# Dealing the glu's two products out between the units of prompt attention

## Chip, cores and metric

The kernel runs on one core of a Trainium2 chip. The metric is the device time of one execution in microseconds (us), the median of several runs. TensorE's clock is granted at one of two levels, 1.2 and 2.4 GHz; the profile writes it as 0.50 and 1.00.

## The reference

Two layers run, one after the other. Each layer handles a prompt of 512 tokens and 8 sample tokens (520 columns in all) with the same weights: a feed-forward half step, the token mixing, and a second half step. The change is in the mixing, which is this:

```python
y_a = (y_ssm @ glu_w) * jax.nn.sigmoid(y_ssm @ glu_v)              # 512 -> 1024 features
attn = attention_fn(q, k, v, q_idx, k_idx, w_idx)
y_b = attn.reshape(bsz, t_len, D_ATT) @ w_branch_attn              # 512 -> 1024 features
mixed = (jax.nn.sigmoid(gate_a) * y_a + jax.nn.sigmoid(gate_b) * y_b) @ w_out
```

`y_ssm` is there before attention begins. Prompt attention is over 512 tokens and 8 heads of 64, with an indexer that keeps the best 128 keys of each query. Sample attention is over 2048 cached keys, of which 256 are gathered for each sample.

## The kernel before

All activations are feature major: 128 features on the partitions, 520 tokens along the row, in two halves of 260 columns (one PSUM bank each; the tile `PS` is four pairs of banks). An fp32 product `x @ w` is made of three fp32r products, hi*hi, hi*lo and lo*hi. Weights come in chunks through a ring of four slots: SyncE loads `stage` (`load`), ScalarE writes `w_hi`, VectorE writes the rest `lo_over` in place of `stage` (the two `split` functions, L714 and L1569), and TensorE's `tile` uses them. A slot is free again when TensorE has used the chunk four before (`chunk_used`). All orders are written out by hand: each engine has its own program, and semaphores tie them.

The mixing's stages, in the order of time: projections and the state space model (its outputs `y_hi`, `y_lo`, the gates in `gT`), the v product, the index scores and the choice of keys, prompt attention, the tail of sample attention, the glu and branch stage, the output projection `wo`.

Prompt attention has 32 units n: four query tiles t of 128 tokens by eight heads, with t + 1 key tiles. TensorE's order (L1503 on) is `logits(n + 2)` (`PS<-kT,qT`), `turn_scaled(n)` (`PS<-dgr,ex`, the transposed, scaled weights), `values(n - 1)` (`PS<-pT,vP`). VectorE does `lowered` (mask and maximum, L2192) and `scaled_diagonal` (`dgr`, L2202), ScalarE `exps` (L998) and the copy `turned_out` (`pT`, L1006). Beside eight of the units (`sample_beside`, n = 6, 9, ... 27) VectorE multiplies gathered keys of one sample by that sample's query (`key_logits`, `prk`, L2177), which TensorE has spread over all partitions with one fp32 matmul into PSUM pair 3 (`spread_query`, `PS<-q_s,pick`).

The glu and branch stage begins at `att_s_ready`, when the sample's attention rows are done; SyncE then also reloads `xT` (2 MB) from memory. In each of eight output blocks there are three tiles of 24 matmuls, glu_w, glu_v and branch:

```python
for v in range(12):
    ...
    tile(v % 4, [(chunk('glu', v, i, 12), 0, KD // 2, P)], (h_hi, h_lo) if v % 3 == 2 else (y_hi, y_lo),
         first=KD // 2 if v % 3 == 2 else 0)
```

ScalarE takes the sigmoid of the glu_v tile (L1040), VectorE makes the four elementwise steps (L2277 to L2285), ScalarE rounds the sum to `mx_hi` (L1043) and VectorE writes `mx_lo` (L2289). The output projection waits for all eight `mx_lo`.

## Time and profile before

| | |
|---|---|
| median of 3 runs | 3499.21 us (3491.34 to 3499.61) |
| the profiled execution | 3497.53 us, its span 3495.8 us |
| TensorE matmul busy | 2979.6 us, 85% of the span |
| VectorE, ScalarE, GpSimd busy | 47%, 37%, 10% |
| granted TensorE clock, mean | 0.888 |
| prompt attention, layer one | 1036.5 to 1146.4 us |
| tail of sample attention | 1146.4 to 1173.8 us |
| glu and branch | 1173.8 to 1252.7 us |

The profile is that of one execution. PE is TensorE, DVE VectorE, ACT ScalarE, POOL GpSimd and SP SyncE. Matmuls overlap in their records, so two that start 0.24 us apart can each be listed with 0.28 us; the start to start distance is what a group costs. An fp32 matmul is two records. In a row of the timeline, what stands in brackets is the idle time of the engine before it and who ended it.

### The profile page before, as it was taken

The numbers are of one execution on the slowest core, as the hardware profiler recorded it, in microseconds if no ns is written. First come the engines' busy times: TensorE is split into PE (matmuls) and PEld (weight loads), VectorE is DVE, ScalarE is ACT, GpSimd is POOL, SyncE is SP. The second block draws the span as 40 slices with busy tenths as digits, with TensorE's granted clock in tenths as the row PEclk, the third lists the DMA queues.
The fourth block names the chain that finished last, engine by engine and source line by source line (L and its number), as shares of the span: only waits on it lengthen the run. The fifth ranks groups of instructions, "written<-read, shape, count | busy, mean of one in ns | idle before, by whom it ended". The sixth has DMA issues, their size and how long they took to land. (4 is left out here: it accounts for less than half of the span.)

```text
span 3495.8 us, 56227 instructions
## 1 busy us (share of the span) xinstructions
PE 2979.6 (85%) x21838; PEld 2754.9 (79%) x21838; DVE 1650.8 (47%) x3202; ACT 1276.4 (37%) x2050; POOL 332.7 (10%) x309
## 2 busy tenths in 40 slices
PE   5999996698839987999769999957887499799996
PEld 4899996687715787999759999957886257789996
DVE  4542446665385444323464424476644844443234
ACT  5542334334252234322165323243443422343221
POOL 2000002032031101000010000020320310100000
PEclk8999997899956998999879999978998579899998
DMA  7443533122201332232164435330221113322321
GB/s 230 123 148 103 156 100 123 31 55 55 74 18 38 114 99 61 84 97 83 38 206 145 144 109 155 97 114 26 54 61 62 30 37 116 86 73 84 100 79 52
DMA packets 450149, 319.80 MB, mean 91 GB/s; under 512 B 24841, under 2 KB 403073, under 8 KB 449210
## 3 DMA queue, kind: packets, MB, share of 16 engines
q1 hardware_dynamic: 444570, 292.37, 28.2%
q0 software_dynamic: 5408, 25.17, 2.3%
q8 instruction: 105, 1.72, 0.2%
q14 instruction: 66, 0.54, 0.1%
HBM read 306.28 MB, written 11.21 MB: 91 GB/s over the span
## 5 line engine op out<-in xcount | busy, mean ns | idle before, releaser
L1067 PE MATMUL PS<-h_hi,w_hi 128*128 128x260 f32 (+1 forms) x4000 | 838.2, 291 | 41.3 <-DVE h_lo L1637 35.0
L1067 PE MATMUL PS<-h_lo,w_hi 128*128 128x260 f32 (+1 forms) x4000 | 816.3, 286 | 0.0
L1569 DVE TENSOR_TENSOR lo_apart<-stage,w_hi 128x1024 fp32r<-128x1024 f32 (+2 forms) x448 | 495.4, 1141 | 467.2 <-ACT w_hi L714 459.6
L1067 PEld LDWEIGHTS PS<-h_hi,w_hi 128*128 128x128 f32 (+1 forms) x4000 | 631.8, 192 | 63.1 <-issue 39.6
L1067 PEld LDWEIGHTS PS<-h_lo,w_hi 128*128 128x128 f32 (+1 forms) x4000 | 628.2, 192 | 0.0
L714 ACT ACTIVATE w_hi<-stage 128x1024 fp32r<-128x1024 f32 (+3 forms) x586 | 541.1, 955 | 96.5 <-DMA stage<-in_mod_w 33.0
L1067 PE MATMUL PS<-h_hi,lo_apart 128*128 128x260 f32 x2816 | 568.7, 284 | 0.0
L1067 PEld LDWEIGHTS PS<-h_hi,lo_apart 128*128 128x128 f32 x2816 | 436.9, 189 | 0.0
L1067 PE MATMUL PS<-hid_lo,w_hi 128*128 128x260 f32 x1408 | 286.2, 285 | 0.0
L1067 PE MATMUL PS<-hid_hi,w_hi 128*128 128x260 f32 x1408 | 285.6, 284 | 0.0
L1067 PE MATMUL PS<-hid_hi,lo_apart 128*128 128x260 f32 x1408 | 285.2, 284 | 0.0
L1685 DVE TENSOR_TENSOR hidf<-sil,PS 128x520 f32<-128x520 f32 x88 | 61.3, 696 | 406.2 <-PE PS L1067 406.2
L1067 PE MATMUL PS<-h_hi,lo_over 128*128 128x260 f32 (+1 forms) x1184 | 248.0, 292 | 0.0
L789 ACT ACTIVATE hid_hi<-hidf 128x520 f32 (+1 forms) x88 | 56.2, 639 | 466.1 <-DVE hidf L1685 466.1
L1067 PEld LDWEIGHTS PS<-hid_hi,lo_apart 128*128 128x128 f32 x1408 | 219.4, 190 | 0.0
L1067 PEld LDWEIGHTS PS<-hid_hi,w_hi 128*128 128x128 f32 x1408 | 219.3, 190 | 0.1
L1067 PEld LDWEIGHTS PS<-hid_lo,w_hi 128*128 128x128 f32 x1408 | 219.2, 190 | 0.0
L1569 DVE TENSOR_TENSOR lo_over<-stage,w_hi 128x1024 fp32r<-128x1024 f32 (+1 forms) x138 | 143.0, 1041 | 130.1 <-ACT w_hi L714 129.1
L1067 PEld LDWEIGHTS PS<-h_hi,lo_over 128*128 128x128 f32 (+1 forms) x1184 | 191.7, 197 | 0.0
L2324 POOL COPY ssum<-sq 128x520 f32<-128x520 f32 x6 | 6.5, 1085 | 1694.0 <-ACT sq L729 1694.0
L1067 PE MATMUL PS<-w_hi,c_st 128*128 128x512 f32 x288 | 127.6, 443 | 18.8 <-DVE lo_apart L1569 11.3
L783 ACT ACTIVATE sil<-PS 128x520 f32<-128x520 f32 x88 | 53.2, 605 | 199.3 <-PE PS L1067 199.1
(408 smaller groups left out, 4058.0 us busy)
## 6 DMA issues: line engine op xcount, KB each, us to landing
stage<-in_ffn_in SPq DMA_DIRECT2D x176, 512.0 KB, 4.0
stage<-in_mod_w SPq DMA_DIRECT2D x144, 512.0 KB, 4.8
stage<-in_w_in SPq DMA_DIRECT2D x72, 512.0 KB, 3.8
stage<-in_ffn_out SPq DMA_DIRECT2D x64, 384.0 KB, 3.7
stage<-in_ffn_out SPq DMA_DIRECT2D x64, 320.0 KB, 3.5
stage<-in_w_out SPq DMA_DIRECT2D x16, 512.0 KB, 4.0
x_hold<-xT SPq DMA_DIRECT2D x2, 2080.0 KB, 6.8
xT<-x_hold SPq DMA_DIRECT2D x2, 2080.0 KB, 8.9
```

What stands on the lines that cost most here:

```text
L714: nc.scalar.activation(w_hi[:, ch.slot, 0:ch.elems], stage[:, ch.slot, 0:ch.elems], ACT.Copy)\
L783: nc.scalar.activation(sil[:, m, :].rearrange("p (a n) -> p a n", a=2), PS[:, 2 * m, :, 0:HALF], ACT.Silu).then_inc(ev_a, 1)
L789: nc.scalar.activation(hid_hi[:, bass.ds(i * 2 + m, 1), :], hidf[:, m:m + 1, :], ACT.Copy)\
L1067: return nc.tensor.matmul(out, lhsT, rhs, start=start, stop=stop)
L1569: nc.vector.tensor_tensor(lows(ch)[:, ch.slot, 0:ch.elems], stage[:, ch.slot, 0:ch.elems], w_hi[:, ch.slot, 0:ch.elems].bitcast(FP32), ALU ...
L1685: nc.vector.tensor_tensor(hidf[:, m, :].rearrange("p (a n) -> p a n", a=2), sil[:, m, :].rearrange("p (a n) -> p a n", a=2), PS[:, up, :, ...
L2324: pool.tensor_copy(ssum[:], sq[:, 0, :]).then_inc(sq_added, 1)
```

## The change

The chunk phase 'glu' keeps only the two glu weights (16 chunks), and a new phase 'br' has the 8 branch chunks. After each attention unit n TensorE runs `fill(n)`: one half (260 columns) of one of the two products of block n // 4, 12 matmuls, into PSUM pair 3. Units 4m and 4m + 1 make the product with glu_w, units 4m + 2 and 4m + 3 that with glu_v, into the same two banks. VectorE multiplies the first into `gT` (`gated_by_gate`, in unit 4m + 2), ScalarE takes the sigmoid of the second (`sigmoids`, in unit 4m + 4), VectorE multiplies that in as well (`gated_by_sigmoid`, in unit 4m + 5). The splits of the chunks stand in the even units. The queries of the samples no longer go through TensorE: SyncE writes `q_s` to memory and reads each row back, spread over the partitions, into `qb`. SyncE's loads of the first four glu chunks stand ahead of the outputs of the states. The branch stage has eight tiles with three elementwise steps each. Besides, some semaphores are merged and one increment (`hf_ready`) goes.

```diff
-            ('glu', 24, 4 * P, 8, 16), ('wo', 8, BLK, 8, 0),
+            ('glu', 16, 4 * P, 0, 0), ('br', 8, 4 * P, 0, 8), ('wo', 8, BLK, 8, 0),
...
+                def glu_pair(m):
+                    for q, name in enumerate(('glu_w', 'glu_v')):
+                        load(chunk('glu', 2 * m + q), rows_of(name, 0, KD // 2, m * P, P))
+
                 def out(name, src, view, sent=out_done):
                     sp.dma_start(view(io[name][lds]), src).then_inc(sent, 16)
 
+                glu_pair(0)
+                glu_pair(1)
...
+                sp.dma_start(q_hold, q_s[:]).then_inc(q_held, 16)
+
+                def query(b):
+                    if b >= 4:
+                        sp.wait_ge(kg_used, b - 3)
+                    sp.dma_start(qb[:, b % 4, :], q_hold[b:b + 1, :].partition_broadcast(P)).then_inc(qb_in[b % 4], 16)
+
+                sp.wait_ge(gi_ready, 1)
+                sp.wait_ge(q_held, 16)
+                for b in range(4):
+                    query(b)
+                glu_pair(2)
+                glu_pair(3)
+                for m in range(4, KD):
+                    query(m)
+                    glu_pair(m)
...
-                def branches(i):
-                    for m in range(4):
-                        for q, name in enumerate(('glu_w', 'glu_v', 'w_branch_attn')):
-                            load(chunk('glu', 3 * m + q, i, 12), rows_of(name, 0, KD // 2, (i * 4 + m) * P, P))
-                        if type(i) is int and i == m == 0:
-                            sp.wait_ge(att_s_ready, 1)
-                            sp.dma_start(xT[:].rearrange("p k n -> p (k n)"), x_hold).then_inc(x_back, 16)
-                branches(0)
-                branches(1)
+                sp.wait_ge(att_s_ready, 1)
+                sp.dma_start(xT[:].rearrange("p k n -> p (k n)"), x_hold).then_inc(x_back, 16)
+                for m in range(3, KD):
+                    branch(m)
...
+                def sigmoids(m):
+                    act.wait_ge(chunk_used, chunk('glu', 2 * m + 1).number(1))
+                    if m:
+                        act.wait_ge(part_ready, m)
+                    nc.scalar.activation(sg[:], PS[:, 3, :, 0:HALF], ACT.Sigmoid).then_inc(sig_ready, 1)
+
                 exps(0)
                 for n in range(NU):
                     if n + 1 < NU:
                         exps(n + 1)
                     turned_out(n)
+                    if n % 2 == 0:
+                        split(chunk('glu', n // 2 + 2))
+                    if n % 4 == 0 and n:
+                        sigmoids(n // 4 - 1)
                     if n % H == 2 and n > H:
                         attended(n // H - 1)
                 attended(TT - 1)
+                sigmoids(KD - 1)
...
-                        act.wait_ge(ev_d, i * 8 + (evicts_d['glu'] + 2 * (m - 1)))
-                        nc.scalar.activation(tmpn[:, m % 2, :].rearrange("p (b n) -> p b n", b=2),
-                                             PS[:, (3 * m + 1) % 4, :, 0:HALF], ACT.Sigmoid).then_inc(ev_a, 1)
...
+                for m in range(KD):
+                    split(chunk('br', m + 2))
+                    act.wait_ge(mixf_ready, m + 1)
+                    nc.scalar.activation(mx_hi[:, m:m + 1, :], sq[:, m % 2:m % 2 + 1, :], ACT.Copy).then_inc(mx_hi_ready, 1)
...
-                def spread_query(b):
-
-                    if b >= 2:
-                        pe.wait_ge(kg_used, b - 1)
-                    mm(PS[:, 3, b % 2, :], pick[:, b, :], q_s[:]).then_inc(qb_done, 1)
+                def fill(f):
+                    m, q = divmod(f, 4)
+                    which, half = q // 2, q % 2
+                    ch = chunk('glu', 2 * m + which)
+                    if which:
+                        pe.wait_ge(glu_used, m + 1)
+                    elif m:
+                        pe.wait_ge(sig_ready, m)
+                    pe.wait_ge(lo_done, ch.number(1))
+                    for k in range(KD // 2):
+                        for w, x in ((w_hi, y_hi), (w_hi, y_lo), (lows(ch), y_hi)):
+                            last = mm(PS[:, 3, half, 0:HALF], w[:, ch.slot, k * P:(k + 1) * P], x[:, k, half * HALF:(half + 1) * HALF],
+                                      start=(k == 0 and w is w_hi and x is y_hi), stop=(k == KD // 2 - 1 and w is not w_hi))
+                    if half:
+                        last.then_inc(chunk_used, 1)
...
+                    fill(n)
                 values(len(units_) - 1)
 
                 pe.wait_ge(att_lo, TT)
+                pe.wait_ge(sig_ready, KD)
...
-                with pe.Fori(0, 2) as i:
-                    ea, ed = evicts_a['glu'], evicts_d['glu']
-                    for v in range(12):
-                        pe.wait_ge(ev_a, i * 4 + (ea + (v - 2) // 3))
-                        pe.wait_ge(ev_d, i * 8 + (ed + (v - 4) // 3 + (v - 6) // 3 + 2))
-                        tile(v % 4, [(chunk('glu', v, i, 12), 0, KD // 2, P)], (h_hi, h_lo) if v % 3 == 2 else (y_hi, y_lo),
-                             first=KD // 2 if v % 3 == 2 else 0)
+                for v in range(KD):
+                    if v >= 4:
+                        pe.wait_ge(ev_d, evicts_d['br'] + v - 3)
+                    tile(v % 4, [(chunk('br', v), 0, KD // 2, P)], (h_hi, h_lo), first=KD // 2)
...
-                    dve.wait_ge(qb_done, b + 1)
-                    nc.vector.tensor_tensor(prk[:], kv[b % K_BUFS][:], PS[:, 3, b % 2, :].unsqueeze(1).to_broadcast([P, 2, DA]), ALU.mult)\
+                    dve.wait_ge(qb_in[b % 4], 16 * (b // 4 + 1))
+                    nc.vector.tensor_tensor(prk[:], kv[b % K_BUFS][:], qb[:, b % 4, :].unsqueeze(1).to_broadcast([P, 2, DA]), ALU.mult)\
...
+                def gated_by_gate(m):
+                    dve.wait_ge(chunk_used, chunk('glu', 2 * m).number(1))
+                    g = halves_of(gT[:, m:m + 1, :])
+                    nc.vector.tensor_tensor(g, g, PS[:, 3, :, 0:HALF], ALU.mult).then_inc(glu_used, 1)
+
+                def gated_by_sigmoid(m):
+                    dve.wait_ge(sig_ready, m + 1)
+                    dve.wait_ge(glu_used, m + 1)
+                    g = halves_of(gT[:, m:m + 1, :])
+                    nc.vector.tensor_tensor(g, g, sg[:], ALU.mult).then_inc(part_ready, 1)
+
                 lowered(0)
                 for n in range(TT * H):
                     if n + 1 < TT * H:
                         lowered(n + 1)
                     scaled_diagonal(n)
+                    if n % 2 == 0:
+                        split(chunk('glu', n // 2 + 2))
+                    if n % 4 == 2:
+                        gated_by_gate(n // 4)
+                    if n % 4 == 1 and n > 4:
+                        gated_by_sigmoid(n // 4 - 1)
                     if n in sample_beside:
                         key_logits(sample_beside[n])
                     if n % H == 4 and n > H:
                         attended(n // H - 1)
                 attended(TT - 1)
+                gated_by_sigmoid(KD - 1)
...
+                for m in range(KD):
+                    split(chunk('br', m + 2))
+                    dve.wait_ge(chunk_used, chunk('br', m).number(1))
+                    nc.vector.tensor_tensor(hf[:, m % 2, :].rearrange("p (b n) -> p b n", b=2), PS[:, m % 4, :, 0:HALF],
+                                            halves_of(gT[:, m + KD:m + KD + 1, :]), ALU.mult).then_inc(ev_d, 1)
+                    dve.wait_ge(ev_d, evicts_d['br'] + m + 1)
+                    dve.wait_ge(part_ready, KD)
+                    nc.vector.tensor_tensor(sq[:, m % 2], hf[:, m % 2], gT[:, m, :], ALU.add).then_inc(mixf_ready, 1)
+                    dve.wait_ge(mixf_ready, m + 1)
+                    dve.wait_ge(mx_hi_ready, m + 1)
+                    nc.vector.tensor_tensor(mx_lo[:, m:m + 1, :], sq[:, m % 2:m % 2 + 1], mx_hi[:, m:m + 1, :].bitcast(FP32),
+                                            ALU.subtract).then_inc(mx_lo_ready, 1)
+
```

In the rows of the order that follow, L numbers of "now" are lines of the changed file. ScalarE in prompt attention, units 2 to 5 of t = 0: `ex` is `exps`, `pT` is `turned_out`, `w_hi` a split, `sg` the sigmoid. Before:

```order
L998 ACTIVATE ex,att_140<-lg,att_140 128x128 [waits pt_turned,neg_ready]
L1006 ACTIVATE pT<-PS 128x128 [waits pv_done,pt_turned]
L998 ACTIVATE ex,att_140<-lg,att_140 128x128 [waits pt_turned,neg_ready]
L1006 ACTIVATE pT<-PS 128x128 [waits pv_done,pt_turned]
L998 ACTIVATE ex,att_140<-lg,att_140 128x128 [waits pt_turned,neg_ready]
L1006 ACTIVATE pT<-PS 128x128 [waits pv_done,pt_turned]
```

Now:

```order
L1031 ACTIVATE pT<-PS 128x128 [waits pv_done,pt_turned]
L741 ACTIVATE w_hi<-stage 128x512 [waits chunk_used,stage_full1]
L1042 ACT_TABLE_LOAD
L1042 ACTIVATE sg<-PS 128x520 [waits chunk_used]
L1023 ACT_TABLE_LOAD [waits pt_turned]
L1023 ACTIVATE ex,att_140<-lg,att_140 128x128 [waits neg_ready]
L1031 ACTIVATE pT<-PS 128x128 [waits pv_done,pt_turned]
```

The split, the sigmoid and two table loads now stand between one unit's `pT` and the next but one `ex`. There are eight sigmoids in each layer's attention, each with a load before it, and a load before the exp that follows.

VectorE at unit 6, where the gate product and the first sample's keys meet: `dgr` is the end of `scaled_diagonal`, `prk` the keys by the query. Before:

```order
L2199 RECIPROCAL att_140<-att_140 128x1 [waits ex_ready]
L2202 TENSOR_SCALAR dgr<-ident,att_140 128x128 [waits pt_turned,dve_own]
L2175 ISA
L2177 TENSOR_TENSOR prk<-kv_163,PS 128x1024 [waits qb_done,k_in0]
L2180 TENSOR_REDUCE Lg<-prk 128x16 [waits kg_used]
```

Now:

```order
L2227 RECIPROCAL att_140<-att_140 128x1 [waits ex_ready]
L2230 TENSOR_SCALAR dgr<-ident,att_140 128x128 [waits pt_turned,dve_own]
L1597 TENSOR_TENSOR lo_over<-stage,w_hi 128x512 [waits hi_done]
L2243 TENSOR_TENSOR gT<-gT,PS 128x520 [waits chunk_used]
L2203 ISA
L2205 TENSOR_TENSOR prk<-kv_163,qb 128x1024 [waits qb_in0,k_in0]
L2208 TENSOR_REDUCE Lg<-prk 128x16 [waits kg_used]
```

The split and the gate product now stand behind the diagonal and ahead of the keys; `prk` reads its query from `qb` and no longer from PSUM.

TensorE at unit 4: `kT,qT` is `logits`, `dgr,ex` is `turn_scaled`, `pT,vP` is `values`, and the rows with `y_hi` or `y_lo` begin a fill. Before:

```order
L1067 MATMUL PS<-kT,qT 128x128 [waits neg_ready]
L1067 MATMUL PS<-dgr,ex 128x128 [waits pt_ready,dgr_ready]
L1067 MATMUL PS<-pT,vP 64x128 [waits pt_ready]
L1067 MATMUL PS<-kT,qT 128x128 [waits neg_ready]
L1067 MATMUL PS<-dgr,ex 128x128 [waits pt_ready,dgr_ready]
```

Now:

```order
L1091 MATMUL PS<-kT,qT 128x128 [waits neg_ready]
L1091 MATMUL PS<-dgr,ex 128x128 [waits pt_ready,dgr_ready]
L1091 MATMUL PS<-pT,vP 64x128 [waits pt_ready]
L1091 MATMUL PS<-y_hi,w_hi 128x260 [waits lo_done,sig_ready]
L1091 MATMUL PS<-y_lo,w_hi 128x260
L1091 MATMUL PS<-y_hi,lo_over 128x260
```

Twelve matmuls now stand behind each values group; the first of a unit 4m waits for the sigmoid of the block before, that of a unit 4m + 2 for the gate product (`glu_used`).

## Rows read from the trace of the kernel before

**Rows 1.** Windows: start:end, length, busy us (records) of five engines, PEclk, DMA share, GB/s

```profile
1036.50:1108.00 71.50, 70.67 (x191) 40.79 (x190) 33.83 (x122) 18.95 (x66) 14.72 (x16) 0.50 0.21 59
1108.00:1146.40 38.40, 36.99 (x209) 24.29 (x207) 20.77 (x61) 14.61 (x34) 5.67 (x6) 0.99 0.15 42
...
1173.80:1252.70 78.90, 72.09 (x576) 71.89 (x577) 45.92 (x67) 28.61 (x45) 0.00 (x0) 0.93 0.41 124
2770.60:2842.30 71.70, 70.88 (x191) 40.77 (x190) 33.82 (x122) 18.95 (x66) 14.68 (x16) 0.50 0.20 59
```

**Rows 2.** Timeline (start us, us, engine, line, what), two units t = 0 apart

```profile
2777.86 0.79 PE L1067 MATMUL PS<-kT,qT 64*128 64x128 f32 x2
...
2779.93 0.79 PE L1067 MATMUL PS<-kT,qT 64*128 64x128 f32 x2
```

**Rows 3.** Timeline of TensorE, a unit of t = 1 and a spread query

```profile
1066.58 1.22 PE L1067 MATMUL PS<-kT,qT 64*128 64x256 f32 x2
...
1069.93 2.07 PE L1067 MATMUL PS<-q_s,pick 8*128 8x512 f32 x2
```

**Rows 4.** Timeline at the high clock, a unit of t = 3 with its pT

```profile
1136.78 1.12 PE L1067 MATMUL PS<-kT,qT 64*128 64x512 f32 x2
...
1138.92 1.09 PE L1067 MATMUL PS<-pT,vP 128*64 128x128 f32 x8
...
1139.03 0.60 ACT L1006 ACTIVATE pT<-PS 128x512 f32<-128x512 f32 x1 [1.86 <-PE PS L1067]
...
1139.94 1.16 PE L1067 MATMUL PS<-dgr,ex 128*128 128x128 f32 x8
```

**Rows 5.** Timeline of the glu stage's matmuls, at either clock

```profile
1174.86 0.80 PE L1067 MATMUL PS<-y_hi,w_hi 128*128 128x260 f32 x2 [1.53 <-DVE lo_over L1569]
...
1179.79 0.64 PE L1067 MATMUL PS<-y_hi,lo_over 128*128 128x260 f32 x2
...
1180.22 0.64 PE L1067 MATMUL PS<-y_hi,w_hi 128*128 128x260 f32 x2
...
1183.11 0.40 PE L1067 MATMUL PS<-y_hi,lo_over 128*128 128x260 f32 x2
...
1183.35 0.40 PE L1067 MATMUL PS<-h_hi,w_hi 128*128 128x260 f32 x2
```

**Rows 6.** Windows of 4 us in the stage of the gates

```profile
836.00:840.00 4.00, 2.18 (x28) 1.93 (x28) 3.86 (x14) 0.00 (x0) 0.00 (x0) 1.00 0.00 0
840.00:844.00 4.00, 2.11 (x14) 2.02 (x13) 3.39 (x10) 3.58 (x9) 3.45 (x3) 0.86 0.52 135
```

**Rows 7.** Timeline of TensorE there, the matmul behind the gap

```profile
837.82 0.67 PE L1067 MATMUL PS<-CA,BXl 128*32 128x128 f32 x16 [3.58 <-DVE counting L1795]
```

**Rows 8.** Timeline of the glu stage, a split and the product behind it

```profile
1200.72 0.63 ACT L714 ACTIVATE w_hi<-stage 128x512 fp32r<-128x512 f32 x1 [2.11 <-DMA stage<-in_glu_v]
...
1201.38 0.69 DVE L1569 TENSOR_TENSOR lo_over<-stage,w_hi 128x512 fp32r<-128x512 f32 x1 [2.05 <-ACT w_hi L714]
1201.99 0.69 DVE L2277 TENSOR_TENSOR hf<-tmpn,PS 128x520 f32<-128x520 f32 x1
```

**Rows 9.** Timeline of ScalarE, a table load and the activation behind it

```profile
1174.61 1.28 ACT L714 ACT_TABLE_LOAD   x1
...
1175.91 0.63 ACT L714 ACTIVATE w_hi<-stage 128x512 fp32r<-128x512 f32 x1
```

**Rows 10.** Timeline of VectorE, a sample's keys

```profile
1129.66 1.21 DVE L2177 TENSOR_TENSOR prk<-kv,PS 128x1024 f32<-128x1024 f32 x1
```

**Rows 11.** Timeline of VectorE in the glu stage, sum, mx_lo and split

```profile
1204.53 0.70 DVE L2285 TENSOR_TENSOR sq<-hf 128x520 f32<-128x520 f32 x1
1206.01 0.70 DVE L2289 TENSOR_TENSOR mx_lo<-sq,mx_hi 128x520 fp32r<-128x520 f32 x1 [0.78 <-ACT mx_hi L1043]
1206.62 1.32 DVE L1569 TENSOR_TENSOR lo_over<-stage,w_hi 128x512 fp32r<-128x512 f32 x2
```

**Rows 12.** Timeline of ScalarE, the first glu chunk behind the reload of x

```profile
1183.24 1.38 ACT L714 ACTIVATE w_hi<-stage 128x512 fp32r<-128x512 f32 x2 [6.70 <-DMA stage<-in_glu_w]
```

136 lines of the change are left out of this document (52 added, 84 removed).

## Prediction

> **What bounds the kernel now.** I read the page's busy shares first (TensorE 85%, in the table ahead, so every stage is first asked for its TensorE time), then the windows of the stages that the change touches, then their instructions in order of time. Prompt attention runs 32 units (four query tiles t = 0 to 3, eight heads), and in it TensorE's records leave no gap: 70.67 of 71.50 us, then 36.99 of 38.40 [rows 1]. But in the first 71.5 us the granted clock is 0.50, the level of 1.2 GHz, and only then 0.99, that of 2.4 GHz; layer two shows the same (71.7 us at 0.50). The stage of glu and branch is 78.9 us with 576 matmuls, at 0.93. So the change moves 384 of 576 matmuls out of a dense stage into one that has no TensorE gap to fill, but half of which runs at the low level. Three questions decide: does the clock rise earlier, what do the added handoffs cost, and how short is what is left of the branch stage?
>
> **Prices on TensorE.** At 1.2 GHz a unit of t = 0 (logits, transposing product, values) takes 2.07 us [rows 2], one of t = 1 1066.58 to 1069.93 = 3.35 us [rows 3]. The difference of 1.28 us is the columns of one key tile, the rest, 0.79 us, the starts of three groups. At 2.4 GHz a unit of t = 3 takes 3.16 us [rows 4]: columns at half price, 4 x 0.64 = 2.56, leave 0.60 for the starts. So a unit costs 0.64(t+1) + 0.60 at the high level. All 32: 8 x (0.64 x 10 + 4 x 0.60) = **70.4 us**. A fill is 12 of the glu's matmuls. Two of them take 0.43 us at the low level and 0.24 at the high one [rows 5], so a fill is 2.60 or **1.44 us**, 32 fills 83 or **46 us**. The spread queries go: 2.07 us each by the record at the low level [rows 3], eight per layer, of which two stand before the first unit.
>
> **The clock.** In the branch stage it rose 5.6 us after dense matmuls of this very shape began (1174.86; the pair at 1179.79 still takes 0.43 us, that at 1183.11 0.24 [rows 5]). In attention it stayed low for 71 us, with group starts that take 0.79 of 2.07 us. A fill is 2.60 us without such gaps, and then 2.07 us with them. I take the rise in the first two units. They then cost 2 x 2 us more less what is hidden: 3.2 us. Does it fall again at the handoffs? From 836 to 840 TensorE is busy 2.18 of 4 us at 1.00 [rows 6], just behind an idle gap of 3.58 us [rows 7], and the clock falls only in the next four (0.86). My gaps are 1.6 to 2.5 us with at least 5 us of work between. I let it stay up.
>
> **Two handoffs in every four units.** Both glu products use the same two PSUM banks, so a fill has to wait for who empties them.
> (1) The fill of unit 4m+2 waits for VectorE's product with the gate. VectorE has put a split ahead of that, which waits for ScalarE's half of the split, which stands behind the copy pT of the same unit, which waits for TensorE's transposing product. From the start of the values group: pT starts 0.11 us later [rows 4], takes 0.28 to 0.60; ScalarE's split adds 0.57, VectorE's 0.61 (1201.38 to 1201.99), the product 0.69 [rows 8], and 0.07 to TensorE: 2.05 + pT. The values group covers 0.38, 0.59, 0.80 or 1.02 us of it. Left: 1.95, 1.84, 1.74, 1.63; two of each: **14.3 us**.
> (2) The fill of unit 4m waits for the sigmoid, which stands behind pT, the split and a table load. The load takes 1.28 us, and the next activation starts 1.30 us after it [rows 9]. From the start of the values group: 0.11 + pT + 0.57 + 1.30 + 0.60 + 0.05 = 2.63 + pT, less the values group: 2.2 to 2.6, mean 2.4; seven of them: **17 us**. The second load (back to exp) lies beside the fill and the next logits and costs nothing; if that cover went it would be 1.3 us each.
> On these two waits everything on TensorE is queued, the next logits first. VectorE's sample keys (1.21 us for the product and as much for the sum [rows 10]) come right behind the gate product in units 6 and 18, and near it in two others: 3.7 us of late diagonals. Start and end of the stage as before: 1.3 + 1.4 us. The last sigmoid with its table load: 1.2 us more before the sample's softmax, and 0.7 us for VectorE's product behind it.
>
> Attention then: 70.4 + 46 + 14.3 + 17 + 3.7 + 1.3 + 1.4 + 1.2 + 3.2 = **158.5 us**; before, 1036.5 to 1146.4 = 109.9 [rows 1]. That is **+48.6** per layer, +0.7 behind it, and -0.2 because VectorE waits a little less for the first logits.
>
> **The branch stage** is 8 tiles of 24 matmuls, 2.9 us each. VectorE is slower. Per tile: product to sum 0.73 us (0.70 and a start), sum to mx_lo (with ScalarE's mx_hi between, VectorE idle 0.78) 1.48, mx_lo to split 0.61 [rows 11], split to product 0.61 [rows 8]: **3.43 us**. Tile 0 starts at 1173.9 at 1.2 GHz and is done at 1179.1. The fourth chunk is queued behind the reload of x. In before the chunk that was queued there was split only at 1183.24, after 6.70 us of waiting for it [rows 12]. I take the same: the second product at 1184.5, the last one 6 x 3.43 + 1.8 (two chunks of twice the size) later at 1206.9, its mx_lo ended 2.9 us after: 1209.8. The output projection begins there, before it began at 1252.7: **-42.8**, and +0.8 since TensorE has then been idle some 8 us and starts low (before, a shorter gap). Bounds: TensorE alone would need 23 + 2.6 + 2.9 = 28.5 us, another 7.5 less; a chunk that comes 3 us late adds 3.
>
> **Without price.** Queries by DMA: 16 KB out and eight broadcasts of 256 KB, asked for one to four keys ahead, while DMA stands at 0.21 [rows 1]; an arrival late by 1 us would cost 1 us in eight units. SP is moved: two glu pairs now stand ahead of the outputs of states, and wait until the last chunk of v is used. VectorE waits for these outputs only after ScalarE has copied v out and TensorE has turned the keys, so they have that time to land; bounds 0 and 2 us per layer, I take 0. Chunks 4 to 15 are asked for some two units (5 us and more) before ScalarE splits them. The split of the first four is in the v stage, where VectorE and ScalarE idle. The fp32 activation merges and renamed semaphores change nothing.
>
> **Sum.** Per layer 48.6 + 0.7 - 0.2 - 42.8 + 0.8 = +7.1 us, two layers +14.2. Profiled execution 3497.5 + 14.2 = 3511.7; the median of before stands 1.7 above that execution, so **3513 us**. What I cannot read from the trace: a fill may also pay a group's start (0.2 x 32 = +6.4 per layer), the logits behind it may lose theirs (-6.4), the handoffs may be 0.2 us off each (3), the branch chain 3. Own range 3498 to 3530.
>
> **Rivals.**
> A. The forecast, 68%.
> B. The clock does not rise with the first fills. Per unit that costs 4.67 - 2.68 = 2.0 us at t = 0 and 2.6 at t = 1. Low through t = 0: +12 per layer, 3537; through t = 1: +29, 3571. For it: 71 us at 0.50 under unbroken records. Against: what broke them were group starts, and fills have none. 14%.
> C. A table change costs more than its row. The row shows 1.28 us and no gap around it [rows 9]. 5%, +19 us for seven exposed changes in two layers, 3532; that price is bounded by a second load of the same length in each.
> The Trainium skill ("ScalarE: Activation LUTs", What ACT_TABLE_LOAD costs) says that exp and sigmoid sit in different sets, that a change is 1.28 us and a drain of 1.38 besides, and that activations are to be batched by set, which this change undoes. The row agrees with 1.28 and shows no drain.
> D. Faster. TensorE loads the weights of the fp32 groups behind a fill, so the 0.60 us of starts per unit vanish: 32 x 0.60 x 2 = 38 us, 3475. It decides above 0.36 us per unit (forecast to 10.5 us below the median). For it: only starts stop TensorE in [rows 2 to 4]. Against: two of the three groups in a unit still follow an fp32 group, and each waits for a semaphore. 6%.
> The Trainium skill ("TensorE: Matmul & The Clock Gate", Part 2, step by step) has the queue pull weight loads ahead of running matmuls when row groups don't conflict or the background buffer is free, which would favour D; the starts in [rows 2 to 4] do not show it between fp32 groups.
> E. The freed slots come too late and each of chunks 4 to 15 is waited for by 1 us (glu chunks were waited for by 2.11 us in the old stage [rows 8]): +24, 3537. 7%.
>
> **Chances.** A measurement of this kernel tells 0.3%, 10.5 us, from no change. A lies within it with 25 of its 68 points and above with 43. Faster 6 (D), same 25, slower 43 + 14 + 5 + 7 = 69. For 8 in 10 the range goes from 3490 to 3560: D below and the worse half of B above are left out.
>
> **What will show it.** Right: clock near 1.0 from the first units; ScalarE with 14 more table loads per layer; TensorE idle in attention some 35 us per layer, on the gate product (1.8 each) and on the sigmoid (2.4 each); attention 159 us; from the sample's last row to the output projection 36 us, VectorE's step 3.4 us. Wrong: a clock of 0.50 beyond 15 us, stalls on stage loads, or handoffs under 1.3 us, which would mean that ScalarE and VectorE run ahead of where I put them.

## The result and the profile after

The changed kernel takes **3554.9 us** (median of 4 runs, 3550.3 to 3558.2) against 3495.8 us for the kernel before beside it (4 runs, 3491.3 to 3499.6): a ratio of 1.0168, 95% interval 1.0149 to 1.0188, 59 us slower. The forecast was 3513 us: right in direction, inside the wide range (3490 to 3560) but outside the prediction's own one (3498 to 3530), and 42 us short in size.

The profiled execution of the changed kernel has a span of 3553.0 us, before 3495.8. First the windows of layer one, of the kernel after; they answer to [rows 1] (start:end, length, busy us and records of TensorE, its weight loads, VectorE, ScalarE, GpSimd; granted clock, DMA share, GB/s). The first is prompt attention from VectorE's first logits to the first matmul behind the last unit, then four stretches of it, then the branch stage.

```profile
1034.90:1219.00 184.10, 148.76 (x765) 115.30 (x765) 73.32 (x213) 67.79 (x140) 19.95 (x22) 0.82 0.21 64
1040.00:1058.00 18.00, 13.71 (x62) 10.76 (x63) 5.38 (x24) 5.64 (x15) 0.95 (x1) 0.77 0.26 87
1058.00:1074.00 16.00, 14.15 (x56) 10.61 (x55) 6.93 (x20) 4.25 (x13) 1.90 (x2) 0.63 0.17 50
1074.00:1119.00 45.00, 36.65 (x161) 29.21 (x160) 18.07 (x49) 15.57 (x32) 3.79 (x4) 0.69 0.20 59
1119.00:1219.00 100.00, 79.95 (x476) 60.93 (x475) 40.27 (x107) 40.16 (x73) 9.48 (x10) 0.94 0.18 53
...
1246.00:1284.00 38.00, 25.07 (x196) 23.86 (x197) 23.18 (x35) 11.39 (x18) 0.00 (x0) 0.91 0.46 147
```

The same window of the kernel before, first logits to first matmul behind, is this:

```profile
1037.30:1146.40 109.10, 106.86 (x394) 64.57 (x393) 54.05 (x181) 33.56 (x100) 19.86 (x21) 0.67 0.19 54
```

So attention went from 109.1 to 184.1 us: **+75.0**, where the prediction had +49.3 (48.6, and 0.7 behind the last unit). TensorE's records leave 35.3 us open, as forecast. What was not forecast stands in the last columns: the clock is at 1.00 in none of the first three stretches. Over the 184 us its mean is 0.82; the levels are 0.5 and 1, so about 2 x 0.18 x 184 = 66 us were spent at the low one.

The waits of TensorE on the two handoffs, over the whole execution (waiting line <- releaser: us in total, times, longest us), the changed kernel:

```profile
PE PS L1091 <- ACT sg L1042: 34.4, 14, 3.1
...
PE PS L1091 <- DVE gT L2243: 27.0, 16, 1.9
...
PE PS L1091 <- DVE mx_lo L2325: 16.9, 2, 8.5
```

That is 2.46 us for each sigmoid and 1.69 for each gate product; the prediction had 2.4 and 1.8. The handoffs were sized right. What follows on them was not. TensorE in layer one of the changed kernel, at the first handoffs (start us, us, engine, line, what, idle before):

```profile
1048.01 0.39 PE L1091 MATMUL PS<-y_hi,w_hi 128*128 128x260 f32 x1 [1.85 <-DVE gT L2243]
1048.23 0.28 PE L1091 MATMUL PS<-y_lo,w_hi 128*128 128x260 f32 x1
1048.35 0.32 PE L1091 MATMUL PS<-y_hi,lo_over 128*128 128x260 f32 x1
1048.47 0.42 PE L1091 MATMUL PS<-y_hi,w_hi 128*128 128x260 f32 x1
1048.69 0.42 PE L1091 MATMUL PS<-y_lo,w_hi 128*128 128x260 f32 x1
...
1052.33 0.39 PE L1091 MATMUL PS<-y_hi,w_hi 128*128 128x260 f32 x1
1052.55 0.28 PE L1091 MATMUL PS<-y_lo,w_hi 128*128 128x260 f32 x1
1052.67 0.28 PE L1091 MATMUL PS<-y_hi,lo_over 128*128 128x260 f32 x1
```

Behind 1.85 us of idle time a fill begins at 0.12 us per matmul, and with its fourth matmul the step is 0.22: the clock has fallen to the low level. At 1052.33 it is high again, and behind the next handoff it falls once more. Counted fill by fill over layer one, 16 of 32 fills run at the high level through (about 1.64 us each), 13 with at least nine of their twelve matmuls at the low one (up to 2.90), 3 in between; all 32 take 69.0 us, where the prediction had 46 and two low ones.

The branch stage, from its first matmul to the output projection, and VectorE's chain in it, of the changed kernel:

```profile
1246.83 0.51 PE L1091 MATMUL PS<-h_hi,w_hi 128*128 128x260 f32 x2 [0.51 <-DVE h_lo L2311]
...
1283.68 0.80 PE L1091 MATMUL PS<-mx_hi,w_hi 128*128 128x260 f32 x2 [8.45 <-DVE mx_lo L2325]
```

```profile
1262.36 0.70 DVE L2322 TENSOR_TENSOR sq<-hf,gT 128x520 f32<-128x520 f32 x1
1263.83 0.70 DVE L2325 TENSOR_TENSOR mx_lo<-sq,mx_hi 128x520 fp32r<-128x520 f32 x1 [0.78 <-ACT mx_hi L1069]
1264.45 0.69 DVE L1597 TENSOR_TENSOR lo_over<-stage,w_hi 128x512 fp32r<-128x512 f32 x1
1265.06 0.69 DVE L2318 TENSOR_TENSOR hf<-PS,gT 128x520 f32<-128x520 f32 x1
1265.78 0.70 DVE L2322 TENSOR_TENSOR sq<-hf,gT 128x520 f32<-128x520 f32 x1
```

36.9 us instead of the 78.9 of [rows 1], and a step of 3.42 us from sum to sum (1262.36 to 1265.78). TensorE is idle for 8.45 us ahead of the output projection.

From the first logits to the output projection the two layers take 215.4 and 215.1 us before, 248.8 and 248.0 after: 33 us more in each. All the rest together is 9 us shorter; the start of attention lay between 1030.4 and 1040.4 us in the profiles of all the kernels below, so a few us of that are no effect of a kernel.

### The profile page after: what moved, and what is told of

Read it like the earlier page. It is cut to its first block and busy times, and to the rows that moved or that the text cites. A ratio compares the mean times of both kernels' runs of the same rounds, so it can differ in the third digit from the quotient of the medians.

```text
span 3553.0 us, 56157 instructions
## 1 busy us (share of the span) xinstructions
PE 2956.0 (83%) x21806; PEld 2752.0 (77%) x21806; DVE 1647.3 (46%) x3202; ACT 1314.9 (37%) x2078; POOL 334.1 (9%) x309
## 5 line engine op out<-in xcount | busy, mean ns | idle before, releaser
L1091 PE MATMUL PS<-y_hi,w_hi 128*128 128x260 f32 x256 | 94.1, 367 | 61.4 <-ACT sg L1042 34.4
L1091 PE MATMUL PS<-w_hi,c_st 128*128 128x512 f32 x288 | 127.2, 442 | 18.1 <-DVE lo_apart L1597 10.6
```

What stands on the lines that cost most here:

```text
L1091: return nc.tensor.matmul(out, lhsT, rhs, start=start, stop=stop)
```

## Experiments

Theory 1: the missing 42 us are the granted clock, which falls because TensorE stands idle at the handoffs, and then takes several us of dense work to rise. Theory 2, its rival: the clock is low because of the short fp32 groups of t = 0 and 1, as it was before [rows 1], and the handoffs only stand beside it; then no repair of the handoffs brings it back. Every ratio is against the kernel before, run beside it. On the chips used, that kernel's median lay between 3489.6 and 3495.8 us, so a difference between two runs can be off by up to 6 us in their times; where it matters, it is also given by the ratios (0.01 is 35 us).

**Without handoffs.** The fills stay, nobody empties their banks.

```diff
                 def fill(f):
-                    if which:
-                        pe.wait_ge(glu_used, m + 1)
-                    elif m:
-                        pe.wait_ge(sig_ready, m)
                     pe.wait_ge(lo_done, ch.number(1))
...
-                    if n % 4 == 0 and n:
-                        sigmoids(n // 4 - 1)
...
-                    if n % 4 == 2:
-                        gated_by_gate(n // 4)
-                    if n % 4 == 1 and n > 4:
-                        gated_by_sigmoid(n // 4 - 1)
...
```

> The changed kernel with the fills of attention left in place and split, but nobody empties their two banks between them: the seven sigmoids and the products with gate and sigmoid of the first seven pairs are left out, and so are the waits for them. All 384 matmuls, the splits and the loads are still there. Theory 1 (the granted clock falls because TensorE stands idle at the handoffs): the direct gaps go (34 + 27 us for both layers in the waits, 31 per layer) and so do the falls of the clock, some 22 us per layer; attention 183 -> about 130 us, kernel about 3449 us. Theory 2 (the clock is low because of the group starts of the short units, as in the first 71 us of attention before; the handoffs only stand beside it): only the gaps go, attention about 152 us, kernel about 3493 us, and the clock still falls to 0.50 in the units t = 0 and 1.

Measured 3483.0 us (7 runs, 3468.1 to 3490.4), ratio 0.9962 (0.9947 to 0.9977); attention 147.8 us at a mean clock of 0.90. Neither number came. Fills 2 to 6 are all at the high level, which speaks against theory 2, but then TensorE stops for another reason. TensorE, and what VectorE did in that time, of this run:

```profile
1062.96 0.70 PE L1087 MATMUL PS<-kT,qT 64*128 64x256 f32 x2
1066.30 0.79 PE L1087 MATMUL PS<-dgr,ex 128*128 128x128 f32 x2 [2.64 <-DVE dgr L2222]
...
1067.64 0.58 PE L1087 MATMUL PS<-y_hi,w_hi 128*128 128x260 f32 x1
1068.02 0.42 PE L1087 MATMUL PS<-y_lo,w_hi 128*128 128x260 f32 x1
```

```profile
1061.90 0.69 DVE L1589 TENSOR_TENSOR lo_over<-stage,w_hi 128x512 fp32r<-128x512 f32 x1 [3.37 <-ACT w_hi L741]
1062.51 1.22 DVE L2197 TENSOR_TENSOR prk<-kv,qb 128x1024 f32<-128x1024 f32 x1
1063.77 1.22 DVE L2200 TENSOR_REDUCE Lg<-prk 128x16 f32<-128x1024 f32 x1
```

VectorE waits 3.37 us for ScalarE's split, which stands behind pT of the same unit, and then does split, a sample's product and its sum in one go: 3.1 us. The diagonal `dgr`, without which TensorE cannot transpose, is 2.64 us late, and the fill behind it is at the low level (0.22 per matmul). In the changed kernel the handoffs hid this third wait.

**The gaps filled.** All handoffs stay; TensorE does useless matmuls while it waits.

```diff
                     ch = chunk('glu', 2 * m + which)
+                    if half == 0 and f:
+                        for _ in range(12 if which else 20):
+                            mm(PS[:, 1, (f + 1) % 2, 0:HALF], y_hi[:, 0, 0:P], y_hi[:, 1, 0:HALF])
                     if which:
```

> The changed kernel with every handoff kept, and the idle time filled: ahead of each of the 15 waits TensorE runs matmuls of the fill's own shape that nobody uses, 12 before the wait for the gate product (1.44 us at the high clock), 20 before the wait for the sigmoid (2.4 us), into a bank that is free there. Theory 1: the clock stays at 1.00 once it has risen, and the low stretches, some 22 us per layer, go: attention 183 -> about 161 us, kernel about 3511 us although more work is done. Theory 2: nothing is gained, since the waits end when they did: 3555 us, or up to 20 us more where the added matmuls run past the wait at the low clock.

Measured **3521.3 us**, ratio 1.0080 (1.0063 to 1.0097): 33.6 us less than the changed kernel (31 by the ratios), with 236 more matmuls per layer (1001 against 765) and no handoff taken away. Windows of this run:

```profile
1034.90:1046.00 11.10, 10.32 (x40) 8.51 (x40) 3.47 (x20) 2.96 (x12) 4.76 (x6) 0.54 0.66 234
1046.00:1066.00 20.00, 19.57 (x131) 16.37 (x130) 9.01 (x28) 7.75 (x19) 0.59 (x1) 1.00 0.14 41
1066.00:1074.00 8.00, 6.68 (x27) 4.56 (x25) 2.19 (x11) 2.02 (x7) 1.30 (x2) 0.69 0.42 128
1074.00:1201.10 127.10, 122.21 (x807) 98.68 (x807) 58.23 (x155) 55.40 (x104) 13.27 (x14) 0.99 0.20 59
```

The clock rises in the first 11 us and stays but for one dip, behind a diagonal 1.32 us late. That shows theory 1: the idle time itself costs what TensorE cannot do in it, and some 17 us per layer more. (The expectation was 3511; the dip and matmuls that run past the end of a wait may be the 10 us, which was not separated.)

**Only the sigmoid's gaps filled** (the same edit with `and not which`).

> As the run that filled every gap, but only the seven gaps per layer at the sigmoid (2.2 to 3.0 us) are filled, with 20 matmuls each; the eight at the gate product (1.5 to 1.9 us) stay idle. If the falls of the clock come from the long gaps alone, this gives all that filling both gave: 3521 us, and the clock is high behind the gate's gaps. If gaps of 1.5 to 1.9 us make it fall as well, the falls at t = 0 and 1 stay in part: 3530 to 3550 us.

Measured 3523.4 us, ratio 1.0096 (1.0079 to 1.0112): by the ratios 6 us above filling all (2 by the times of two chips), with intervals that overlap, and 25 of the 31 us gained. In the trace 1.85 us of idle time at the gate product of unit 2 are still followed by two low fills (window 1050 to 1058 at 0.57), the same 1.85 at unit 6 by none, and those of 1.74 at units 10 and 14 by fills of 2.81 and 2.78 us, low nearly throughout. So the gaps at the sigmoid make most of the loss, and the shorter ones are not free.

**The sigmoid by tanh**, which in this run needs no table load beside exp: none is left in attention.

```diff
-                    nc.scalar.activation(sg[:], PS[:, 3, :, 0:HALF], ACT.Sigmoid).then_inc(sig_ready, 1)
+                    nc.scalar.activation(sg[:], PS[:, 3, :, 0:HALF], ACT.Tanh, scale=0.5).then_inc(sig_ready, 1)
...
-                    nc.vector.tensor_tensor(g, g, PS[:, 3, :, 0:HALF], ALU.mult).then_inc(glu_used, 1)
+                    nc.vector.scalar_tensor_tensor(g, g, 0.5, PS[:, 3, :, 0:HALF], ALU.mult, ALU.mult).then_inc(glu_used, 1)
...
-                    nc.vector.tensor_tensor(g, g, sg[:], ALU.mult).then_inc(part_ready, 1)
+                    nc.vector.scalar_tensor_tensor(g, sg[:], 1.0, g, ALU.add, ALU.mult).then_inc(part_ready, 1)
```

> The changed kernel with the sigmoid written as 0.5 (1 + tanh(x/2)): ScalarE computes the tanh, VectorE's two products take the 0.5 and the + 1. Prediction under test: the sigmoid's wait holds one table load of 1.3 us on the path. If tanh needs no change of table beside exp, the 14 or more loads per layer go, the waits for the sigmoid fall from 2.4 to about 1.1 us, 9 us per layer, and the last sigmoid another 1.3. Theory 1 (clock falls at the long gaps): a gap of 1.1 us is shorter than that of the gate, so the falls become fewer too, up to 15 us per layer more: 3505 to 3535 us. Theory 2: 3534 us. If tanh brings a table change of its own: 3555 us.

Measured **3515.6 us**, ratio 1.0071 (1.0051 to 1.0091); attention 159.8 us, clock 0.93: inside theory 1's 3505 to 3535, where theory 2 had 3534. TensorE's waits in this run:

```profile
PE PS L1091 <- DVE gT L2243: 27.0, 16, 1.9
PE PS L1091 <- ACT sg L1042: 14.7, 14, 1.6
PE PS L1091 <- DVE dgr L2230: 10.3, 10, 1.9
```

The sigmoid's waits fell by 19.7 us in 14, 1.41 each: a table load and little besides. The kernel gained 39 us (34 by the ratios). TensorE's waits as a whole fell by only 12.7, since late diagonals, 3.3 us in the changed kernel, are 10.3 now. The rest, some two thirds of the gain, goes with the clock (0.93 against 0.82), as theory 1 has it.

**Each bank emptied by itself**, a unit of attention after it was filled.

```diff
                     if which:
-                        pe.wait_ge(glu_used, m + 1)
+                        pe.wait_ge(glu_used, 2 * m + half + 1)
                     elif m:
-                        pe.wait_ge(sig_ready, m)
+                        pe.wait_ge(sig_ready, 2 * (m - 1) + half + 1)
...
+                    if n % 4 == 0 and n:
+                        sigmoids(n // 4 - 1, 1)
                     if n % 2 == 0:
                         split(chunk('glu', n // 2 + 2))
-                    if n % 4 == 0 and n:
-                        sigmoids(n // 4 - 1)
+                    if n % 4 == 3:
+                        sigmoids(n // 4, 0)
...
```

> The changed kernel with each of the two banks emptied by itself, one unit of attention after it was filled: the gate product of bank 0 in unit 4m+1 and of bank 1 in 4m+2, the sigmoid of bank 0 in unit 4m+3 and of bank 1 in 4m+4, both of the latter ahead of the split. Nothing is left out, there are 16 sigmoids and about 14 more table loads per layer. A handoff has a unit of slack (at least 2.7 us at the high clock against 2.05 to 2.6 of chain). Theory 1: gaps and falls of the clock mostly go, attention 130 to 140 us, kernel 3449 to 3470 us, below the kernel before. Theory 2: gaps go, clock stays: about 3500 us. Rival: two table loads (2.6 us) in every second unit make ScalarE late with exp and pT; then each of 16 units waits 1 to 1.5 us on ScalarE, 3480 to 3500 us with the clock high between.

Measured 3510.1 us, ratio 1.0046 (1.0028 to 1.0063). No wait is left on either handoff, but 46.4 us in 20 waits on diagonals, up to 5.0. The rival held, and cost more than its figure: with sixteen sigmoids ScalarE changes tables 30 times in attention, is 88 of 158 us busy, and exp comes late. It shares this with the late diagonals that the run without handoffs had found.

**The same with tanh.**

> The run with the banks emptied one by one, and the sigmoid by tanh besides; the splits and keys stand as in the changed kernel. All handoffs of the banks are then as good as free, and ScalarE has no table loads that delay exp. What is left is what the run without handoffs showed: VectorE waits for ScalarE's split behind pT in every even unit, has no lead left, and its split with a sample's product and sum makes diagonals late by 2.2 to 2.9 us in four units, with the clock low behind the first two. 3478 to 3492 us, as that run (3483 us). If instead the late diagonals came from something that run alone had, it is near 3445 us.

Measured 3484.8 us (10 runs), ratio 0.9974 (0.9963 to 0.9984), as the run without handoffs (0.9962), and with the same kind of waits: 25.8 us on diagonals, up to 3.2 (there 21.7, up to 2.9). The third wait is confirmed, and so is the mean clock of 0.90 that it costs.

**The split ahead of pT**, one line moved on ScalarE in the changed kernel.

```diff
                     if n + 1 < NU:
                         exps(n + 1)
-                    turned_out(n)
                     if n % 2 == 0:
                         split(chunk('glu', n // 2 + 2))
+                    turned_out(n)
```

> The changed kernel with one move: ScalarE's split of a chunk stands ahead of its copy pT of the same unit, not behind it. Then VectorE's split no longer waits for TensorE's transposing product, and the gate product behind it is done about 1.2 to 1.5 us earlier; the sigmoid comes 0.57 us earlier. By the prediction's two chains the gate's gap falls from 1.5 to 1.9 us to 0.3 to 0.7, the sigmoid's from 2.4 to 1.8; 13 us less idle per layer. With theory 1 the falls of the clock become fewer too, up to 17 us more: 3555 - 2 x 13 to 30 = 3495 to 3529 us. VectorE also keeps its lead of a unit, so the diagonals behind a sample's keys come less late. Rival: pT is later by ScalarE's 0.57 us in 16 units and moves the values; then 9 us per layer come back, and it is 3530 us or above.

Measured **3490.9 us** (10 runs), ratio 1.0003 (0.9991 to 1.0014): 58 us by the ratios for one move (64 by the times of two chips), no worse than the kernel before, and at the low end of the 3495 to 3529 that was expected (3497 by the ratio). The gate product no longer stops TensorE at all, late diagonals are 0.5 us in total, and 25.5 us in 14 waits are left on the sigmoid. The clock still falls behind these:

```profile
1054.15 0.59 PE L1091 MATMUL PS<-y_hi,w_hi 128*128 128x260 f32 x1 [1.92 <-ACT sg L1042]
...
1059.12 0.58 PE L1091 MATMUL PS<-y_hi,w_hi 128*128 128x260 f32 x1
1059.50 0.42 PE L1091 MATMUL PS<-y_lo,w_hi 128*128 128x260 f32 x1
```

Of its seven gaps at the sigmoid in layer one (1.58 to 2.03 us), three are followed by a fill that is low throughout (1.92, 2.03 and 1.81), one by a fall inside the fill (1.70), three by none (1.92, 1.80 and 1.58).

**Tanh and the split ahead together.**

> The changed kernel with two small edits, and the banks emptied together as in it: the sigmoid by tanh, and ScalarE's split ahead of pT. The run with the split moved left no gap at the gate product and 1.6 to 2.0 us at each of seven sigmoids per layer, with the clock low behind four of them. Without the table load (1.28 us) these gaps become 0.3 to 0.7 us. Theory 1: nothing makes the clock fall any more; 32 units 70.4, 32 fills of 1.64 us 52.5, seven gaps 3.5, ends and first rise 7: 134 us of attention against 184, kernel about 3455 us. Theory 2: 3491 - 2 x 9 = 3473 us.

Measured **3454.6 us**, ratio 0.9879 (0.9859 to 0.9899): theory 1's 3455, not theory 2's 3473. Attention takes 131.7 us at 0.96; 30 of 32 fills are high, only the first two are not. By the ratios the two edits gave 34 and 58 us alone and 101 together (39, 64 and 100 by the times).

**The sample's keys in odd units**, product and sum in two units one after the other, on top of that.

```diff
-    sample_beside = {6 + 3 * b: b for b in range(DEC)}
+    sample_beside = {n: b for b, n in enumerate((7, 11, 13, 15, 19, 21, 23, 27))}
...
```

> As the run with the tanh and the split moved, and the sample's keys in odd units with product and sum in two units one after the other. If VectorE has its lead of a unit back by the moved split alone, this gives nothing more (within 5 us of that run); if the diagonals behind the keys were still late there, up to 10 us.

Measured 3450.4 us, ratio 0.9872 (0.9852 to 0.9893): 4 us less than the run before, which the intervals don't tell from nothing. The moved split had already given VectorE its lead back.

**Everything, with the banks one by one.**

> All remedies in one kernel that computes the whole reference: each bank of the fills is emptied by itself a unit later; the sigmoid is 0.5 (1 + tanh(x/2)), so that no table changes; ScalarE's split stands ahead of pT; the sample's keys stand in odd units, product and sum in two units one after the other. The run without handoffs still showed TensorE idle 2.2 to 2.9 us in units 6, 12, 18 and 24 behind VectorE's split and a sample's product and sum, and the clock low behind the first two. Theory 1: no gap over 0.5 us is left, the clock rises in the first units and stays; 32 units 70 us and 32 fills of 1.64 us make 123, with the first rise and both ends 130 us of attention against 183; kernel 3555 - 2 x 53 = 3450 us, below the kernel before. Rival: the diagonals or exponentials are still late somewhere and the clock falls with each: 3465 to 3490 us.

Measured **3443.0 us**, ratio 0.9871 (0.9854 to 0.9887). Theory 1 gave 3450; the kernel before was 6 us faster on this chip than beside the changed kernel, and by the ratio this is 3451. It is also the ratio of the run before it (0.9872): emptying the banks one by one gave nothing more that the times can show. Attention in this run:

```profile
1030.40:1155.70 125.30, 123.09 (x765) 95.34 (x765) 73.80 (x221) 47.57 (x132) 19.88 (x22) 0.98 0.31 95
```

TensorE's records leave 2.2 us open and the clock is 0.98. Against the 109.1 us of before, 32 fills of 1.64 us (52.5) have cost 16 us of attention, since the rest is paid back by the clock, which before was at 0.50 for 71 us, and by the spread queries that are gone.

**Two fills in a row.** The kernel with tanh, split ahead and keys moved, and on TensorE:

```diff
-                    fill(n)
+                    if n % 2:
+                        fill(n - 1)
+                        fill(n)
```

> The run with tanh, the split ahead of pT and the keys in odd units, with one more move on TensorE alone: no fill in even units, both fills of a pair one after the other in the odd one. It tests the price of a fill's start (0.2 us that the prediction left out of its sum and held as a bound): the second fill of a pair follows the first without another group between, so 16 of 32 starts go, 3.2 us per layer, and emptying the banks has two logits, a transposing product and a values group more to hide in, so the sigmoid's gaps of 0.4 to 0.8 us go too, 3.8 us per layer. 3450 - 2 x 7 = 3436 us. If the start belongs to each fill and not to the change of group, 3443 us. Rival: the units between stand closer together and exp and diagonals, which had the fill as cover, come late in even units: 3450 us or above.

Measured **3440.7 us**, ratio 0.9855 (0.9838 to 0.9871); attention 123.1 us, 7.7 less than the 130.8 of the run that it was made from, where 7 were expected. The kernel as a whole is 10 us below that run, 6 by the ratios, where 14 were expected if only a change of group costs a start and 7 if each fill does, so the time does not tell the two apart. The rows do. Those at such a pair:

```profile
1052.16 0.39 PE L1091 MATMUL PS<-y_hi,w_hi 128*128 128x260 f32 x1
1052.38 0.28 PE L1091 MATMUL PS<-y_lo,w_hi 128*128 128x260 f32 x1
...
1053.46 0.28 PE L1091 MATMUL PS<-y_lo,w_hi 128*128 128x260 f32 x1
1053.58 0.28 PE L1091 MATMUL PS<-y_hi,lo_over 128*128 128x260 f32 x1
1053.70 0.28 PE L1091 MATMUL PS<-y_hi,w_hi 128*128 128x260 f32 x1
...
1055.00 0.28 PE L1091 MATMUL PS<-y_hi,lo_over 128*128 128x260 f32 x1
1055.21 0.70 PE L1091 MATMUL PS<-kT,qT 64*128 64x256 f32 x2
```

The first matmul behind an fp32 group takes 0.22 us to the next and the last one 0.21 to the logits, all others 0.12, and the thirteenth (1053.70), which begins the second fill, is no exception. So the start belongs to the change of group, 0.2 us for a fill between two fp32 groups, and a second fill behind a first has none.

**The queries alone**: the kernel before with the DMAs of the change in place of the spread products (its semaphores are merged as in the changed kernel).

```diff
+                sp.dma_start(q_hold, q_s[:]).then_inc(q_held, 16)
+                sp.wait_ge(gi_ready, 1)
+                sp.wait_ge(q_held, 16)
+                for b in range(DEC):
+                    if b >= 4:
+                        sp.wait_ge(kg_used, b - 3)
+                    sp.dma_start(qb[:, b % 4, :], q_hold[b:b + 1, :].partition_broadcast(P)).then_inc(qb_in[b % 4], 16)
...
-                spread_query(0)
-                spread_query(1)
...
-                        spread_query(sample_beside[n - 2] + 2)
...
```

> The kernel before with one part of the change alone: the sample's queries are written to DRAM and spread by eight DMAs of 256 KB instead of TensorE's spread products; the glu and branch stage is untouched (semaphores are merged as in the changed kernel, since the chip has no free ones left). The prediction gave the DMAs no price and each of the spread products 2.07 us at the low clock: six stand in attention behind its first two units and two before it, 16.6 us per layer where TensorE is the bound. Theory 1 (they stood on the path): 3496 - 2 x 12 to 17 = 3462 to 3472 us. Rival (a query or its slot comes late, one to two us in eight units, or the glu's first chunks, now behind the queries on SyncE, come late): 3480 to 3496 us.

Measured **3465.5 us**, ratio 0.9932 (0.9916 to 0.9949): 24 us less than before, 12 per layer. This part of the change is a gain by itself. Six of the eight spread products stood in attention, and 6 x 2.07 = 12.4 us is what it lost (109.1 - 96.5 = 12.6). The two ahead of the first unit ran beside work of VectorE: from the last `rv,oh` product to VectorE's first logits it took 5.5 us with them and 5.2 without. In its attention (96.5 us) the low level lasts as it did before:

```profile
1033.90:1092.00 58.10, 57.32 (x164) 35.29 (x164) 31.72 (x115) 17.49 (x62) 14.21 (x16) 0.50 0.37 121
1092.00:1130.40 38.40, 36.99 (x218) 25.27 (x216) 22.46 (x67) 16.29 (x39) 5.67 (x6) 0.99 0.14 42
```

So the spread products had not held the clock down: it stays low without them under the short fp32 groups, and with fills between the same groups it rises. Dealing out the glu as the change does it therefore cost 24 + 59 = 83 us on top of this kernel; in the best form tried (ratio 0.9855 against 0.9932) it gave some 27 instead.

The runs together (attention of layer one from the first logits to the first matmul behind it; "low" is 2 x (1 - mean clock) x length; us are medians on different chips, so compare the ratios):

| kernel | us | ratio | attention | clock | low, us |
|---|---|---|---|---|---|
| before | 3495.8 | 1 | 109.1 | 0.67 | 72 |
| changed | 3554.9 | 1.0168 | 184.1 | 0.82 | 66 |
| sigmoid's gaps filled | 3523.4 | 1.0096 | 168.8 | 0.93 | 24 |
| all gaps filled | 3521.3 | 1.0080 | 166.2 | 0.95 | 17 |
| tanh | 3515.6 | 1.0071 | 159.8 | 0.93 | 22 |
| banks one by one | 3510.1 | 1.0046 | 157.9 | 0.90 | 32 |
| split ahead | 3490.9 | 1.0003 | 151.4 | 0.89 | 33 |
| banks one by one, tanh | 3484.8 | 0.9974 | 148.3 | 0.90 | 30 |
| no handoffs | 3483.0 | 0.9962 | 147.8 | 0.90 | 30 |
| queries alone | 3465.5 | 0.9932 | 96.5 | 0.70 | 58 |
| tanh, split ahead | 3454.6 | 0.9879 | 131.7 | 0.96 | 11 |
| tanh, split ahead, keys | 3450.4 | 0.9872 | 130.8 | 0.96 | 10 |
| the last, and banks one by one | 3443.0 | 0.9871 | 125.3 | 0.98 | 5 |
| tanh, split ahead, keys, fills in pairs | 3440.7 | 0.9855 | 123.1 | 0.97 | 7 |

The last two beat both kernels, by 1.3 to 1.5% the kernel before and by over 3% the changed one. They were timed on different chips, so their ratios and not their times are to be compared; these do not tell them apart.

## The prediction, point by point

Attention of layer one, term by term. The fills' durations are read from start to next start in the timeline, the units are what remains.

| term, us | forecast | measured |
|---|---|---|
| 32 units | 70.4 | 78.9 |
| 32 fills | 46 | 69.0 |
| clock low in the first two units | 3.2 | (in the two above) |
| eight handoffs at the gate | 14.3 | 13.5 |
| seven at the sigmoid | 17 | 17.3 |
| late diagonals | 3.7 | 1.1 |
| start, end, last sigmoid and product | 4.6 | 4.3 |
| sum | 159.2 | 184.1 |

**The step that failed** is "Does it fall again at the handoffs? ... I let it stay up." It falls: at all seven handoffs of t = 0 and 1 and at two of the eight of t = 2 and 3 (units 20 and 24). Fills and units at the low level account for 69.0 - 32 x 1.64 = 16.5 us and, with 78.9 - 70.4, for another 8.5, less the 3.2 that were in the sum: 22 us per layer. The run with filled gaps gave back some 17 of them per layer with no handoff removed. The argument for it had been one gap of 3.58 us [rows 7], with the clock at 1.00 around it and at 0.86 in the four us behind [rows 6]. Those rows already held the fall; one dip that costs little in a sparse stage was taken for no dip, and then carried over to fifteen places per layer with dense work behind each.

The Trainium skill ("TensorE: Matmul & The Clock Gate", HAM oscillation) describes a kernel in which each wait for a DMA puts the clock back so that the next piece of work starts at the low rate, again and again. The trace of the changed kernel shows the same pattern behind waits for ScalarE and VectorE: 11 of its 30 fills behind the first rise are at the low level, but not behind every wait. The prediction did not weigh this rule.

**The term that was put at nothing**: a fill also pays a group's start. The prediction held it as a bound of +6.4 per layer, outside its sum, and it is 32 x 0.2 = 6.4 (1.64 us a fill, not 1.44). It was readable: the glu stage's matmuls in [rows 5] follow each other without a group between, and every fp32 group in [rows 2 to 4] shows a start. The bound -6.4 (the logits behind a fill lose theirs) did not come: 0.21 us from the last matmul to the logits. These two, 22 + 6.4, less 2.6 us of late diagonals that did not come and 0.8 on the remaining terms, are the 24.9 us per layer between 159.2 and 184.1.

**What was right.** Both handoff chains, to 0.1 us each: 2.46 against 2.4 and 1.69 against 1.8. ScalarE with 14 more table loads per layer: ScalarE's lists show 28 more over both. TensorE idle 35 us per layer in attention: 35.3. The branch stage: 36.9 us against 36, step 3.42 against 3.43, so 42.0 shorter where 42.8 was forecast. The low start of the output projection, put at 0.8, cost 0.2: its first nine groups take 3.91 us, and they took 3.69 before. Together 41.8 against 42.0. The chunk behind the reload of x was late as taken: VectorE waited for it until 1257.60, and the second product began 11.4 us into the stage, where 10.6 were taken. The queries: no late arrival, and the products they replace were worth 12 us per layer on the path, less than the eight times 2.07 us that they took.

**What the sign rested on.** Forecast per layer 48.6 + 0.7 - 42.8 + 0.8 less 0.2 = +7.1; measured +33 from the first logits to the output projection, with 9 us less elsewhere in the execution. All of the difference is in attention.

**The rivals.** A (the clock up after two units and staying): the rise came as forecast, some 10 us after the first logits (right behind the second fill), the staying did not. B (low through t = 0 or t = 1, 3537 or 3571) gave times on both sides of the result, but by another mechanism: a clock that does not rise. It rose and fell. (By the prices beside it, 8 x 2.0 + 8 x 2.6 less the 3.2 in the sum, the second case is +33 per layer and not +29.) C: a table load took 1.28 us and the sigmoid began 1.30 us after its start; nothing besides was seen, and without the loads each of the sigmoid's waits fell by 1.41. The drain of 1.38 us that the Trainium skill ("ScalarE: Activation LUTs", What ACT_TABLE_LOAD costs) adds to a load does not show in any run here. What the same page of the Trainium skill advises under "Table sets: the hidden batching unit", to batch activations by set, does hold in this kernel, in part by way of the clock: 20 us of waits removed at the sigmoid gave 34 to 39. D (starts vanish): the fp32 units kept their starts (1.20 us for one of t = 0 at the high level, where 1.24 was taken), and in the pairs only a fill behind a fill has none. E: the fills waited for nobody's chunks.

**The late diagonals** were sized at 3.7 us by the wrong view. They were 1.1 us here, since the handoffs stopped TensorE while VectorE caught up, and 11 to 13 us per layer as soon as the handoffs were gone. A wait that hides another makes it look cheap.

What stays open: why the clock fell behind some gaps and not behind others of the same length or longer (in the changed kernel a gap of 3.01 us at unit 28 is followed by a fill at the high level, one of 2.32 at unit 24 by a low one). All seven handoffs among the short units of t = 0 and 1 brought a fall, two of the eight among the longer ones did; whether short fp32 groups around a gap help the clock to fall, which would be a part of theory 2, no run separates. Open too are the 9 us by which the execution outside these stretches was shorter.

## What to carry to other kernels

Price a wait on a dense engine twice: by its own length, and by what the clock does to the work behind it; here 31 us of gaps per layer cost about 20 more, and filling them with useless matmuls was worth 31 to 34 us of the kernel. When work is dealt out between units of a pipeline, what matters is where each producer and consumer stands in the order of its engine: one split moved ahead of one copy gave some 60 us, because it took VectorE's split off TensorE's critical product. Free a buffer before it is wanted (one unit ahead took the last handoff waits away here, though the times show no further gain), and put pieces of the same shape next to each other.

## What the runs showed of the hardware

- The granted clock fell to the low level behind some idle gaps of TensorE of 1.3 us (the run with all gaps filled, unit 6) to 5.0 us (banks one by one), and not behind others of up to 3.0 us (the changed kernel, unit 28). In the changed kernel 9 of 15 handoffs were followed by a fall. Once low, one to three fills went by before it was high again. In the kernel with queries by DMA it stayed low for 58 us under short fp32 groups whose records leave 0.8 us open; with twelve dense matmuls between the same groups it rose within 10 us.
- A matmul of 128x260 follows another in 0.12 us at the high level, also into another bank and with other weights (the run with fills in pairs); behind an fp32 group, and ahead of one, the step is 0.22 and 0.21.
- exp and tanh share a table: the kernel with tanh has two loads at exp in attention, where the changed one has 16 there and 16 at the sigmoid (both layers).
